# TensorE's loop runs one step further for the last down product, and the scatters leave the pad rows out by a bounds check

## The reference, cut to what matters

```python
logits = x @ router_w + router_b
top_v, top_i = lax.top_k(logits, 4);  gates = softmax(top_v)
# for each expert e, over the rows that chose it:
hh = xblk @ e_w_in[e] + e_b_in[e]            # 1024 -> 2048
gate, up = split(hh);  gate = min(gate, 7);  up = clip(up, -7, 7)
act = gate * sigmoid(1.702 * gate) * (up + 1)
y[token] += gate_of_token * (act @ e_w_out[e] + e_b_out[e])   # 1024 -> 1024
x = layer_norm(alpha * x + y)
```

## Time and profile before

| | us |
|---|---|
| median of 3 runs | 1586.2 (1585.85 to 1587.4) |
| profiled execution, its own time | 1584.48 |
| its span, first to last instruction | 1582.6 |
| TensorE matmuls busy | 1367.9 (86%) |
| POOL, DVE, ACT busy | 300.1, 489.7, 196.9 |
| mean granted TensorE clock | 0.911 of full speed |
| read from HBM / written | 446.66 MB / 19.42 MB |

### The profile page before, as it was taken

The page is one execution under the profiler, slowest core; times in us unless marked ns, Lnnn a source line. Parts: engine busy times, 40 slices in busy tenths (PEclk is TensorE's granted clock), DMA queues, the critical chain, the costliest instruction groups (busy, mean ns, idle before and its releaser), DMA issues.

```text
span 1582.6 us, 36359 instructions
## 1 busy us (share of the span) xinstructions
PE 1367.9 (86%) x12785; PEld 600.9 (38%) x12786; DVE 489.7 (31%) x1633; ACT 196.9 (12%) x495; POOL 300.1 (19%) x247
## 2 busy tenths in 40 slices
PE   6998879994788979999986998999889999999970
PEld 5885334752232323333331333333333333333320
DVE  2993521337221212222220222222222222222225
ACT  0003231111110101111100111111101111111102
POOL 7000231100120211222220221222112222222223
PEclk9999679775897989999996999999999999999985
DMA  9501513108699799989799999949998769999443
GB/s 314 170 0 40 193 51 120 58 29 363 257 373 416 294 414 415 366 350 409 303 413 421 418 411 414 382 158 411 415 407 349 274 260 352 411 409 413 179 172 111
DMA packets 93495, 463.47 MB, mean 293 GB/s; under 512 B 10676, under 2 KB 37265, under 8 KB 43693
## 3 DMA queue, kind: packets, MB, share of 16 engines
q1 hardware_dynamic: 74315, 432.95, 67.4%
q0 software_dynamic: 16640, 22.30, 6.5%
q10 hardware_dynamic: 2514, 7.88, 1.3%
HBM read 446.66 MB, written 19.42 MB: 294 GB/s over the span
## 4 chain that ended last, share of the span: by engine, by line
PE 58%; DMA 11%; issue 4%; DVE 1%; POOLq 0%; SPq 0%; ACT 0%; POOL 0%; ACTq 0%; DVEq 0%
PE pu L1495 33%; PE py L1507 18%; DMA ring<-in_e_in 11%; PE px L1472 2%; PE pu L1488 2%; PE ph L1479 2%; PE raw L1465 1%; DMA xq<-x_rows,idx 0%; DVE bn L1717 0%; DMA ring<-acc_rows 0%; DVE ring L1733 0%; DVE mv L1727 0%; SPq L214 0%; POOLq L1285 0%; POOL ring L1457 0%
## 5 line engine op out<-in xcount | busy, mean ns | idle before, releaser
L1495 PE MATMUL pu<-ring,xgT 128*32 128x512 f32 x5248 | 619.5, 619 | 52.3 <-DMA ring<-in_e_in 52.3
L1495 PEld LDWEIGHTS pu<-ring,xgT 128*32 128x32 f32 x5248 | 165.3, 112 | 444.5 <-issue 334.3
L1507 PE MATMUL py<-ring,hid 128*32 128x256 f32 x5248 | 305.7, 386 | 11.2 <-issue 11.2
L1423 POOL DMA_INDIRECT acc_rows<-y,idx x82 | 130.9, 1596 | 892.2 <-ACT y L1601 882.1
L1695 DVE TENSOR_SCALAR gg<-pu 128x256 f32<-128x256 f32 x82 | 34.8, 425 | 594.3 <-PE pu L1495 594.3
L1507 PEld LDWEIGHTS py<-ring,hid 128*32 128x32 f32 x5248 | 163.7, 111 | 128.2 <-issue 31.5
L1581 ACT ACTIVATE xgT<-px 128x256 f32<-128x256 f32 x83 | 31.9, 384 | 764.3 <-PE px L1472 764.3
L718 PE MATMUL pair<-xt,ring 128*128 128x260 f32 x448 | 100.3, 387 | 15.5 <-DMA xt<-in_xT 15.5
L1416 POOL DMA_INDIRECT xq<-x_rows,idx x85 | 88.9, 1046 | 52.4 <-DVE idx L1662 27.5
L718 PEld LDWEIGHTS pair<-xt,ring 128*128 128x128 f32 x448 | 86.0, 192 | 28.5 <-DMA xt<-in_xT 15.1
L1644 DVE TENSOR_TENSOR onehot<-rankm,slot_rank 128x160 bf16 (+1 forms) x344 | 88.8, 321 | 1.7
(11 more groups left out here) (233 smaller groups left out, 857.6 us busy)
## 6 DMA issues: line engine op xcount, KB each, us to landing
ring<-in_e_in SPq DMA_DIRECT2D x256, 1024.0 KB, 15.3
ring<-in_e_out SPq DMA_DIRECT2D x128, 1024.0 KB, 16.8
ring<-in_w_in SPq DMA_DIRECT2D x3, 1536.0 KB, 13.1
ring<-in_w_o SPq DMA_DIRECT2D x1, 4096.0 KB, 13.2
ring<-in_w_in SPq DMA_DIRECT2D x6, 512.0 KB, 12.4
xt<-in_xT SPq DMA_DIRECT2D x2, 1040.0 KB, 9.5
xtok<-in_x_prompt POOLq DMA_DIRECT2D x4, 512.0 KB, 3.7
x_rows<-conv ACTq DMA_DIRECT2D x4, 512.0 KB, 8.9
```

The costliest lines, as they stand in the source:

```text
L1423: nc.gpsimd.indirect_dma_start(out=acc_quarters, out_offset=bass.IndirectOffsetOnAxis(ap=idx8[:, c:c + 1], axis=0), in_=y[:, i], in_offset ...
L1495: mm = nc.tensor.matmul(pu[quarter(c)], xgT[:, k], w[:, :, c * QC:(c + 1) * QC], start=False, stop=k == KT - 1, skip_group_check=True)
L1507: mm = nc.tensor.matmul(py[quarter(c), 0:QC], hid[:, 2 * q + f], w[:, f, c * QC:(c + 1) * QC], start=q == 0 and f == 0, stop=q == FT // 2 ...
```

## The change

Four things. (1) TensorE's loop goes one step further, and the last down product is done in it by the same three copies as the others. For this the body is split into three conditional parts: `If(g < last)`, `If(g <= last)` around `run_down`, and `If(g < last)` around `turn_hidden`. (2) `code_of(g)` is read ahead of the first condition, so in every turn, also in those past the last group. (3) `slots(g + 3)` now comes ahead of `run_down(g - 1)`, not behind it. (4) The scatter gets a bounds check, and the 32 extra rows, their memset, their DMA and the waits for them are gone.

```diff
-NROW = R + GS
-    acc_dram = nc.dram_tensor("acc_rows", [NROW, D], F32).ap()
+    acc_dram = nc.dram_tensor("acc_rows", [R, D], F32).ap()
...
-            nc.gpsimd.memset(zero, 0.0).then_inc(zero_made, 1)
...
-            a.wait_ge(zero_made, 1)
-            a.dma_start(acc_dram[PAD0:PAD0 + GS, :].rearrange("r (c n) -> (r c) n", n=QC), zero
-                        ).then_inc(pads_zeroed, 16)
...
-            a.wait_ge(pads_zeroed, 16)
...
-                    in_=y[:, i], in_offset=None, compute_op=ALU.add).then_inc(scattered, 16)
+                    in_=y[:, i], in_offset=None, compute_op=ALU.add,
+                    bounds_check=NQ * R - 1, oob_is_err=False).then_inc(scattered, 16)
...
-            with pe.Fori(1, MAXG) as g:
+            with pe.Fori(1, MAXG + 1) as g:
+                code = code_of(g)
                 with pe.If(g < last):
-                    code = code_of(g)
                     pe.wait_ge(xgT_ready, g + 1)
...
-                    run_down(g - 1, code)
                     pe.wait_ge(slots_read, g + 3)
                     slots(g + 3)
+                with pe.Else():
+                    pe.nop()
+                with pe.If(g <= last):
+                    run_down(g - 1, code)
+                with pe.Else():
+                    pe.nop()
+                with pe.If(g < last):
                     turn_hidden(g)
                 with pe.Else():
                     pe.nop()
-            run_down(last - 1, code_of(last))
```

More of the change, by code:

```diff
@@ L322, in first_block @@
         gT = up[0:NE, 1, 0:P]
-        zero = cpre[:, 0:2].rearrange("p i b t -> p (i b t)")[:, 0:D // 4]
         def chn(name):
@@ L342, in first_block @@
         zeroed = bsem("zeroed")
-        zero_made = bsem("zero_made")
         copied = bsem("state_copied")
@@ L374, in first_block @@
         acc_sent = [bsem(f"acc_sent{i}") for i in range(2)]
-        pads_zeroed = bsem("pads_zeroed")
         sy_done = bsem("sample_values_done")
```

## The result

| | before | after |
|---|---|---|
| median, us | 1586.0 (6 runs) | 1592.3 (6 runs, 1589.99 to 1593.88) |
| ratio of the runs, 95% interval | | 1.0038 (1.0025 to 1.0051) |
| span of the profiled execution | 1582.6 | 1590.8 |

A forecast was written before the change was run, and what follows sets the result against it. Weights set the pace in some stretches, TensorE in the others, with its sequencer making the hole between turns. Turns +26.5, tail -10.4, pads -3, zeroing -0.2: +12.9 us on 1586.2, so 1599 us; range 1585 to 1611.

The forecast's parts named there:

- this walk: TensorE's sequencer work from the branch leaving the down copy to the next turn's first product: 2.8 us, 2.1 covered.
- the walk stays covered: Rival: the sequencer's lead hides the additions at the turn's end, so -13.6 us, 1572.6 us in all; chance 0.12.
- The price of a turn: Turn's end on TensorE: longer walk and shorter cover cost 0.50 us a turn (0.40 to 0.65), +26.5 us in all.
- the jump over the `Else` of `If(g <= last)`: Behind the down product: a jump the change was said to add to TensorE's sequencer work, 0.23 us a turn.
- the lost cover of 0.29: Slots' 0.29 us of TensorE work moves ahead of the down product, so less work hides the sequencer at turn's end.
- How many turns, and which: In the experts' loop, 53 of 79 turns pay; 26 in weight-bound stretches absorb the cost in their waits.
- the stretches that TensorE paces: Four stretches of the experts' loop where loads wait for TensorE to free a slot; their 53 turns pay.
- the saturated ones: Four stretches of the experts' loop where weights set the pace, 408 to 412 GB/s; their 26 turns pay nothing.
- the first three turns: The start of the experts' loop, left out of the forecast's sum.
- a sign of being wrong by the prediction's own words: A hole opening ahead of the down product, where the forecast counted nothing, would show it wrong.
- The tail: After the last group: last down product starts about 1529.9, not 1539.33; ScalarE's empty turns then bind; -10.4 us.
- The pads: GpSimd's scatters: 26.5 pad packets fewer each, paying only in the saturated stretches; -3 us, plus -0.2 for zeroing.

The follow-up runs named there:

- e9: The kernel before's loop with the bounds check, plus code_of(g) read a second time at the end of each TensorE turn: 1621.8 us, ratio 1.0228.
- e5: The changed kernel with one nop added behind run_down inside If(g <= last): 1602.9 us, ratio 1.0114.
- e11: The kernel before's turn with the bounds check, TensorE's loop ending at last, no If around the turn: 1554.4 us, ratio 0.9814.
- e7: e6 with ScalarE's last results also moved into its Else, ahead of its empty turns: 1577.1 us, ratio 0.9953.
- e3: The changed kernel with slots(g + 3) and its wait put back behind the down product, ahead of turn_hidden: 1591.1 us, ratio 1.0029.
- e6: The kernel before's turn with the bounds check, the last down product done in the loop's Else from its own three copies: 1578.8 us, ratio 0.9964.
- e10: e7 with one copy of the last down product instead of three, ring position and counts as constants: 1572.6 us, ratio 0.9915.
- e12: e11 with ScalarE's loop also ending at last and the last down product as one copy with constants: 1550.8 us, ratio 0.9783.

## Why the prediction was right and wrong

**What bounds a turn: right.** "What is put into this walk is paid in time" holds in both directions: e9 adds a read and each turn grows, e5 adds a jump and it grows, e11 takes compare and jump out and the hole closes. The rival *the walk stays covered* fell at once: the hole grew in all 70 turns, and 20 weight loads of the down product were still to come at the branch that leaves the copy, as in the earlier trace rows.

**The price of a turn: wrong, and this is the step that failed.** I took 0.50 us with 0.40 as the least. Measured: 0.20 in 49 of 70 turns, 0.48 in 21, 0.28 in the mean. Two of the term's parts were mis-sized. First, "the jump over the `Else` of `If(g <= last)`, 0.23" is executed only behind the third copy; behind the others it is joined with the jump that leaves the copy (58 instructions, e5). I had taken it that every conditional part closes with a jump of its own. The kernel before did not show it either way: its nested copies leave through one jump each, but both `Else` parts end at the same place there. Second, `slots` costs 0.29 us of the chain behind the down product and 0.19 ahead of it. I had taken it to cost the same in both places, so that the lost cover of 0.29 was a loss in full; 0.10 of it comes back. Put together: +0.29 of cover, +0.02 of walk (a compare and a register operation for two register operations), -0.10 of slots, = 0.2; and the jump on top in a third of the turns.

**How many turns, and which: right.** 53 said, 56 by e9's dose. 53 x 0.28 = 14.9 us against +14.5 seen in the stretches that TensorE paces and +1.3 in the saturated ones. With the price of e5, 53 x 0.47 = 24.9 against +24.5 and +0.1. So the time was off by the price of a turn: 53 x (0.50 - 0.28) = 11.7 us too much. That the total was only 6.6 us too high is in part luck: the first three turns (+1.7), the saturated stretches (+1.3) and the smaller gain of pads and zeroing (about 1) made up for some of it. The four holes ahead of the down product, a sign of being wrong by the prediction's own words, are 2.6 us of the +15.8; it had counted nothing there.

**The tail: right.** -10.4 said, -10.8 measured, ScalarE's empty turns late next (e7 takes them away and gains 1.7), the product at the high clock, the 14 dearer empty turns of TensorE covered: it reached the barrier at 1580.9, GpSimd at 1585.1.

```profile
L1276 PEldq DRAIN  x1: 13/13/13, 1580.9 to 1580.9; - x1
...
L1276 POOLq DRAIN  x1: 5399/5399/5399, 1585.1 to 1585.1; - x1
```

**The pads: right in kind.** -3.2 said with the zeroing, about -2 measured. GpSimd's queue moved 20.08 MB instead of 22.30. The packets are still 16,640: what I announced, 26.5 packets fewer a scatter, was wrong. A pad's packet record is still there, without its bytes.

**The price of one jump.** The jump of 51 ns and the compare of 108 that the Trainium skill gives ("Advanced Engine Details and Errata", Control Flow Timing) would have put the whole at about +1 us. The traces say 163 to 177 ns for most jumps and 63 to 92 for most compares that fall through; what made my sum too large was a jump that isn't executed, not a wrong price for one that is.

**What stays open.** The first three turns of the changed kernel are 1.7 us longer and those of e3, with nearly the same code, 0.4. The granted clock is low from 428.8 to 439.1 in the first and from 430.8 to 437.6 in the second, so the difference goes with the clock; no run was made to show it. Nor does any run show why `slots` is 0.10 us cheaper ahead of the down product, or in which stretch the pads' 2 us are saved.

## What to carry to other kernels

In a loop whose bound is known only on the chip, an engine's sequencer can be the bound between two turns though the engine looks busy: read the hole ahead of the turn's first instruction, and count the sequencer's instructions from the last one that the queue covers. Don't count branches from the source; read them in the trace: here a jump to a jump was joined, and a nop that left no instruction still broke the join. Before an `If` is split to save a tail, see whether the loop can end at the count itself: here that saved the tail and every turn's end, 30 us where the split lost 6.

## What the runs showed of the hardware that was not expected

- A pad row left out by the bounds check saves its bytes (22.30 to 20.08 MB) but no packet record (16,640 in both).
- A loop's first pass had one jump of 5.8 to 6.3 us in every kernel here; more code to jump over added a second (5.5 us in e6, 6.1 in e7), and one copy in place of three took it away (e10). No later pass has one.
- A loop whose end is in a register had no price of its own in the turn: the compare at the loop's end takes 215 ns in e11 as in the kernel before, and the hole is 0.1 us in the mean, the least of the kernels here together with e12.
